# A two-layer decoder trunk: key choice of the first query half moved up, query rotation and four low parts on GpSimd, the first gate blocks as rounded products

## The reference

```python
for i in range(DEPTH):                                   # 2 layers
    p = x @ (w_in0 if i == 0 else w_in_rest[i - 1])      # attention, gates, r/k/v, LoRA inputs
    y_a = dsa_sparse_mqa(...)                            # below
    y_b = rwkv7_time_mix(...)                            # 4 rounds of 4 heads in the kernel
    g_a, g_b = jnp.split(jax.nn.sigmoid(p_gate + b_gate[i]), 2, axis=-1)
    x = layer_norm(alpha * x + (g_a * y_a + g_b * y_b) @ w_out[i], ...)
    x = layer_norm(alpha * x + conv_glu_ffn(x, ...), ...)

def dsa_sparse_mqa(...):
    c_q = rms_norm(cq_raw, g_cq)
    q = partial_rope((c_q @ w_uq).reshape(B, S, H_A, DH_A), *rope_a)      # 8 heads of 128, 32 rotated
    qi = partial_rope((c_q @ w_iq).reshape(B, S, H_IDX, D_IDX), *rope_i)  # 8 index heads of 64
    # per half of 128 queries:
    rel = jax.nn.relu(jnp.einsum('bqhd,bsd->bqhs', qib, ki))
    score = jnp.einsum('bqhs,bqh->bqs', rel, wib)        # weighted sum over the index heads
    _, idx = lax.top_k(score, 64)                        # the key choice
    # softmax attention over the chosen keys, heads of q against one shared k and v
```

## Time and profile before

| | |
|---|---|
| median of 3 runs | 1110.08 us (1109.13 to 1113.75) |
| the profiled execution | 1109.16 us, of it 1107.3 us from the first to the last instruction (span) |
| PE busy | 1077.9 us, 97% |
| DVE, ACT, POOL busy | 802.8, 570.7, 72.2 us |
| mean granted TensorE clock | 0.993 of full |
| PE's longest waits in sum | 4.6 us for the first load, 4.2 us for DVE in 2 layer norms, then 1.6 and less |

### The profile page before, as it was taken

One profiled execution on the slowest core, in us unless ns is written; L12 is line 12 of the kernel. 1 busy time (PEld: TensorE's weight loads), 2 busy tenths in 40 slices (PEclk: granted clock), 3 DMA queues, 4 the chain that ended last, 5 costly groups with the idle time before them and its releaser, 6 DMA issues. The chain is left out here.

```text
span 1107.3 us, 31915 instructions
## 1 busy us (share of the span) xinstructions
PE 1077.9 (97%) x13568; PEld 979.3 (88%) x13568; DVE 802.8 (72%) x1471; ACT 570.7 (52%) x1008; POOL 72.2 (7%) x61
## 2 busy tenths in 40 slices
PE   8999999999999999999999999999999999999996
PEld 8878888888897999998898888888888979999885
DVE  3678787878676877774557887878776778777645
ACT  3653555655444555553246445655565445555531
POOL 0000010101001000000100000101010010000001
PEclk9999999999999999999999999999999999999999
DMA  8533232322574666666374323222316646665661
GB/s 301 165 103 118 75 99 85 100 83 86 191 227 136 209 191 189 187 205 191 131 239 143 116 88 97 89 80 87 97 61 217 222 125 228 185 189 189 210 189 57
DMA packets 45527, 165.58 MB, mean 150 GB/s; under 512 B 5169, under 2 KB 5425, under 8 KB 45137
## 3 DMA queue, kind: packets, MB, share of 16 engines
q1 hardware_dynamic: 42736, 154.03, 43.3%
q0 software_dynamic: 1504, 7.47, 2.3%
q10 hardware_dynamic: 1152, 2.10, 0.6%
HBM read 160.44 MB, written 3.15 MB: 148 GB/s over the span
## 5 line engine op out<-in xcount | busy, mean ns | idle before, releaser
L771 PE MATMUL ps<-x_tok_r,mid_hi 128*128 128x256 f32 x576 | 176.5, 306 | 0.5 <-DVE ring_r L1753 0.5
L773 PE MATMUL ps<-x_tok_r,ring_r 128*128 128x256 f32 x576 | 162.2, 282 | 0.0
L772 PE MATMUL ps<-yb_hi,mid_hi 128*128 128x256 f32 x576 | 162.1, 281 | 0.0
L771 PEld LDWEIGHTS ps<-x_tok_r,mid_hi 128*128 128x128 f32 x576 | 108.6, 189 | 9.3 <-issue 1.4
L1753 DVE TENSOR_TENSOR ring_r<-ring,mid_hi 128x1024 fp32r<-128x1024 f32 x80 | 96.8, 1211 | 19.3 <-ACT mid_hi L1341 19.1
L772 PEld LDWEIGHTS ps<-yb_hi,mid_hi 128*128 128x128 f32 x576 | 108.9, 189 | 0.7 <-issue 0.7
L773 PEld LDWEIGHTS ps<-x_tok_r,ring_r 128*128 128x128 f32 x576 | 108.9, 189 | 0.0
L1341 ACT CAST mid_hi<-ring 128x1024 fp32r<-128x1024 f32 x80 | 83.8, 1047 | 36.5 <-PE ps L773 28.9
L2014 DVE TENSOR_TENSOR rs_ks_r<-ring,tha_kkn_r 128x1024 fp32r<-128x1024 f32 x44 | 53.9, 1225 | 21.5 <-ACT tha_kkn_r L1393 21.5
L2014 DVE TENSOR_TENSOR w_lo<-ring,w_hi 128x1024 fp32r<-128x1024 f32 x42 | 51.5, 1225 | 21.6 <-ACT w_hi L1393 21.5
L2014 DVE TENSOR_TENSOR vs_dC_r<-ring,b_k_r 128x1024 fp32r<-128x1024 f32 x44 | 53.7, 1220 | 17.1 <-ACT b_k_r L1393 17.1
(11 more groups left out here) (487 smaller groups left out, 3373.6 us busy)
## 6 DMA issues: line engine op xcount, KB each, us to landing
ring<-stream_dram SPq DMA_DIRECT2D x281, 512.0 KB, 3.7
lora_w<-lora_dram POOLq DMA_DIRECT2D x2, 1536.0 KB, 7.2
W_bt<-rpar_dram POOLq DMA_DIRECT2D x4, 512.0 KB, 5.7
kt_V<-rpar_dram POOLq DMA_DIRECT2D x4, 512.0 KB, 7.9
x_tok<-x_dram SPq DMA_DIRECT2D x2, 512.0 KB, 4.7
v_saved_dram<-vs_dC ACTq DMA_DIRECT2D x4, 256.0 KB, 4.3
x_tok<-x_dram SPq DMA_DIRECT2D x1, 1024.0 KB, 6.3
vf<-v_saved_dram ACTq DMA_DIRECT2D x4, 256.0 KB, 3.7
```

Of the source, the lines that this page charges most:

```text
L771: pe.matmul(dst, lh, rh, start=start, stop=False)
L772: pe.matmul(dst, lh, rl, start=False, stop=False)
L773: return pe.matmul(dst, ll, rh, start=False, stop=stop)
```

## The change

Four edits, all ahead of round 0 of each layer, and all in both layers.

1. The six first gate blocks are rounded products too. `MIDS` takes them in and `FIRST_MIDS` grows by six. With the last block of v (number 7 of the layer's rounded blocks) the gate blocks are numbers 8 to 13.
2. The low parts of numbers 7 to 10 (`POOL_LOWS`) are made by GpSimd (`low`), the rest by DVE.
3. The rotation of the queries (`queries(0)`, `queries(1)`) goes from DVE to GpSimd, between its low parts 8 and 9.
4. `topk(0)` stands right behind `s0` and `s1` on DVE, ahead of the sums of `s2` to `s5`. Into `topk(1)` go `rkv(l, 0, 2)`, `prep_decay`, `prep_pend`, `prep_ss`, `prep_rn` and a low part. Low part 13 stands between `prep_arc` and `prep_bk`.

```diff
-FIRST_MIDS = 2 + 3 * GB
+FIRST_MIDS = 2 + 3 * GB + 2 * GATES_FIRST
+POOL_LOWS = (7, 8, 9, 10)
...
-MIDS = [s for s in SLOTS if s[1] == "gate" and s[2] >= 2 * GATES_FIRST or s[1] == "rkv" and s[2] % KB >= GB
+MIDS = [s for s in SLOTS if s[1] == "gate" or s[1] == "rkv" and s[2] % KB >= GB
...
+            def low(l, m):
+
+                k = SLOT_AT[MIDS[l * MID_PER_LAYER + m]] % RING
+                pool.wait_ge(*act_mid(l, m))
+                pool.tensor_tensor(rounded["ring"][:, k, :], ring[:, k, :], f32(mid_hi[m % NM][:, :]), ALU.subtract
+                                   ).then_inc(*pool_mid.inc(l, m))
+
+            def queries(l, j):
+
+                pool.wait_ge(*act_att(l, f"q{j}"))
...
+                pool.tensor_tensor(t[0], x1, cos, ALU.mult)
+                pool.tensor_tensor(t[1], x2, sin, ALU.mult)
+                pool.tensor_tensor(t[2], x2, cos, ALU.mult)
+                pool.tensor_tensor(t[3], x1, sin, ALU.mult).then_inc(*pool_att.inc(l, f"rq{j}a"))
+                pool.wait_ge(*pool_att(l, f"rq{j}a"))
+                pool.tensor_tensor(x1, t[0], t[1], ALU.subtract)
+                pool.tensor_tensor(x2, t[2], t[3], ALU.add).then_inc(*pool_att.inc(l, f"rq{j}"))
...
+                low(l, 7)
+                low(l, 8)
+                queries(l, 0)
+                queries(l, 1)
+                low(l, 9)
+                low(l, 10)
                 head_norm(GROUPS * l)
...
-                pe.wait_ge(*dve_att(l, "rq1"))
+                pe.wait_ge(*pool_att(l, "rq1"))
...
-                topk(0)
-                prep_decay(r0)
-                prep_pend(r0)
-                prep_ss(r0)
-                topk(1, lambda: prep_rn(r0))
+                topk(1, {1: [lambda: rkv(l, 0, 2)], 5: [lambda: prep_decay(r0)],
+                         6: [lambda: prep_pend(r0), lambda: prep_ss(r0), lambda: mids_up_to(l, 12)],
+                         7: [lambda: prep_rn(r0)]})
+                mids_up_to(l, 13)
                 prep_keys(r0)
                 prep_keys_scaled(r0)
                 prep_arc(r0)
+                mids_up_to(l, 14)
                 prep_bk(r0)
```

More of the change, by code:

```diff
@@ L496, in trunk, with low_made @@
         act_mid = by_layer("act_mid", list(range(MID_PER_LAYER)))
-        dve_mid = by_layer("dve_mid", list(range(MID_PER_LAYER)))
+        dve_mid = by_layer("dve_mid", [m for m in range(MID_PER_LAYER) if m not in POOL_LOWS])
+        pool_mid = by_layer("pool_mid", list(POOL_LOWS))
+        def low_made(l, m):
+            return (pool_mid if m in POOL_LOWS else dve_mid)(l, m)
         mid_last = mid_gaps()
@@ L530, in trunk @@
         scores = lambda i: [f"s0{h}" for h in range(4 * i, 4 * i + 4)] if i < 2 else [f"s1{h}" for h in (2 * i - 4, 2 * i - 3)]
+        top = lambda t: ([f"causal{t}"] + sum([[f"max{t}{i}", f"rep{t}{i}"] for i in range(8)], [])
+                         + [f"sel{t}", f"selb{t}", f"keep{t}"])
         dve_att = Steps(sem("dve_att"), [["wi", "kst", "kmv"] + rope("rk") + ["cq", "kic", "ki"] + rope("rki") + rope("rqi")
-                                         + scores(0) + scores(1)
-                                         + (scores(2) + scores(3) + rope("rq0") + scores(4) + scores(5) + rope("rq1") if l else
-                                            rope("rq0") + scores(2) + scores(3) + rope("rq1") + scores(4) + scores(5))
-                                         + sum([[f"causal{t}"] + sum([[f"max{t}{i}", f"rep{t}{i}"] for i in range(8)], [])
-                                                + [f"sel{t}", f"selb{t}", f"keep{t}"] for t in range(TT)], [])
+                                         + scores(0) + scores(1) + top(0)
+                                         + scores(2) + scores(3) + scores(4) + scores(5) + top(1)
                                          + sum([[f"lh{g}", f"lg{g}", f"mx{g}", f"rc{g}", f"pn{g}"] for g in range(GROUPS)], [])
                                          for l in L2])
-        pool_att = by_layer("pool_att", ["eps", "rs"])
+        pool_att = by_layer("pool_att", ["eps", "rs"] + rope("rq0") + rope("rq1"))
         pe_prep = Steps(sem("pe_prep"), [(["ss", "zw", "za"] if r % GROUPS else ["zw", "za", "ss"]) + (["zv"] if r >= GROUPS else []) + ["rnT", "rnx"]
@@ L1604, in _ @@
                     index_turned()
+                    mids_up_to(l, 8)
                     scores_of(0)
                     scores_of(1)
+                    mids_up_to(l, 9)
                     queries(0)
@@ L1626, in _ @@
                 for i in range(1, GATES_FIRST):
+                    mids_up_to(l, 11 + 2 * i)
+                    mids_up_to(l, 12 + 2 * i)
                     gate(l, i)
-                    if i == 1:
-                        mids_up_to(l, FIRST_MIDS + 1)
+                mids_up_to(l, FIRST_MIDS + 1)
                 for g in range(GROUPS):
@@ L1748, in mids_up_to @@
             def mids_up_to(l, end):
-                for m in range(dve_mid.next - l * MID_PER_LAYER, min(end, MID_PER_LAYER)):
+                made = dve_mid.next - l * (MID_PER_LAYER - len(POOL_LOWS))
+                for m in [m for m in range(MID_PER_LAYER) if m not in POOL_LOWS][made:]:
+                    if m >= end:
+                        break
                     k = SLOT_AT[MIDS[l * MID_PER_LAYER + m]] % RING
@@ L2256, in scores_of, with topk @@
                         last.then_inc(*dve_att.inc(l, f"s{t}{h}"))
[L2258 to L2290 removed]
+                def topk(t, between={}):
                     dve.wait_ge(*dve_att(l, f"s{t}{H_IDX - 1}"))
@@ L2296, in topk @@
                     for i in range(TOPK // 8):
-                        if i == 5 and halfway:
-                            halfway()
+                        for step in between.get(i, []):
+                            step()
                         dve.wait_ge(*dve_att(l, f"causal{t}" if i == 0 else f"rep{t}{i - 1}"))
@@ L2310, in topk @@
                                       ).then_inc(*dve_att.inc(l, f"keep{t}"))
+                if l:
+                    shift_add(l, ("vres", 0), lora[:, 2:3, :], [26])
+                    index_queries()
+                    mids_up_to(l, 7)
+                    lora_w_low(1)
+                    rkv(l, 0, 1)
+                    lora_w_low(2)
+                    lora_low(2)
+                else:
+                    mids_up_to(l, 7)
+                    index_queries()
+                    lora_w_low(1)
+                    rkv(l, 0, 1)
+                scores_of(0)
+                scores_of(1)
+                topk(0)
+                for i in range(2, 6):
+                    scores_of(i)
                 def o_low(i):
```

56 lines of the change are left out of this document (15 added, 41 removed).

## The result

| | before | changed |
|---|---|---|
| median | 1110.38 us (6 runs, 1108.50 to 1113.83) | 1123.53 us (6 runs, 1120.71 to 1126.23) |
| ratio | | 1.0108, 95% interval 1.0089 to 1.0128 |
| profiled execution | 1109.16 us, span 1107.3 | 1126.23 us, span 1124.4 |
| mean granted clock | 0.993 | 0.990 |

The change makes the kernel about 1% slower; 1124.0 was forecast. So a difference is read between anchors on PE within one stretch, not between the two ends.

What follows compares the result with a forecast made beforehand. PE and DVE, arriving together at the grams 0.3 us apart, bound the kernel. Layer 1 +6.8, layer 0 +5.5, clock +1.7 make 14.0 on 1109.16: 1123.2, median 1124; forecast's own range 1118 to 1131, whole range 1111 to 1131.

Steps and rivals of the forecast that it cites:

- transposes late: Transposes of the queries ahead of round 0 start late: 7.6 us in layer 1, 0.4 in layer 0.
- `prep_1` behind ACT's copies: Layer 0: prep_1 waits to 76.7 for ACT's copies of the transposed queries, so PE stands 4.3 us.
- six blocks, at full clock: First gate blocks on PE: rounded 2.85 us against 3.55 in float32, saving 4.3 us per layer.
- `prep_rnT` behind the power: PE waits for head_norm's power on GpSimd, itself held by a DVE low part: +2.4 us layer 1, +3.2 layer 0.
- low part 13: PE's last gate block waits for DVE's keys, scaled keys, arc and this low part: +1.9 us in each layer.
- clock: Half level of 1.2 GHz after a long PE stand: one loss counted, layer 1's, 1.7 us, bounds 0 and 6.8.
- v: Layer 1: PE's 0.78 us wait for v behind the grams goes, since DVE is ahead by then: -0.8 us.
- The port: GpSimd and two-input DVE operations block each other; DVE's wait, not in the trace, taken as a whole GpSimd operation.
- GpSimd's prices: GpSimd's costs: a 1024-column low part 2.4 us (2.4 to 3.3), a 128-column rotation operation 0.45 (0.3 to 0.6).
- DVE never waits: Rival on the port: only GpSimd waits for DVE; layer 1 +2.4, layer 0 -0.2, time 1114 us; chance 0.13.
- nobody waits: Rival on the port: neither engine waits; layer 0 -2.0, layer 1 +1.0, time 1109 to 1111 us; chance 0.05.
- the blocks' saving arrives whole: Rival on the gate blocks: -4.3 us in both layers and the 0.8 wait gone, 1101 us; chance 0.03.

Runs made afterwards that it cites:

- the experiment with the port alone: Kernel before plus two unused GpSimd subtractions of 1024 columns per layer, one beside the score sums, one beside topk(0)'s MAX8 and MATCH_REPLACE8; 1110.22 us, one run.

## Why the prediction was right, step by step

| term, us | layer 1: forecast, measured | layer 0: forecast, measured |
|---|---|---|
| transposes late | 7.6, 6.0 | 0.4, 0.0 |
| `prep_1` behind ACT's copies | none | 4.3, 3.1 |
| six blocks, at full clock | -4.3, -3.4 | -4.3, -3.4 |
| `prep_rnT` behind the power | 2.4, 1.7 | 3.2, 0.9 |
| low part 13 | 1.9, 1.7 | 1.9, 1.7 |
| clock | 1.7, 2.8 | none, 2.6 |
| v | -0.8, -0.5 | none |

Measured they make 8.3 and 4.9 us, near the 8.3 and 5.1 between the anchors; forecast 14.0 with the clock, measured 13.2. Every wait came where it was named and ended with the engine that was named; only the stand ahead of the transposes was shorter than the 6 to 7 us named as its sign, 4.92. The sum is as good as it is because errors cancel: the lateness and the waits are 6.6 us smaller together, the saving of the blocks 1.8 and that of v 0.3 smaller, the clock 3.7 larger.

**The port** was the open step, and its direction was right: DVE does stand for the whole of a GpSimd low part (1.98 for an operation of 0.29, and the experiment with the port alone). The reading behind it was weaker than it says: the trace of before does have a case where DVE came second, a TENSOR_TENSOR at 305.14 that took its usual 1.22 beside a power of 8 columns (304.01 to 305.66). So it is the low parts for which DVE stands. And the first sum was taken for a two-input operation, which it is not; it waited all the same. Too much was made of it in one place: the rotation's small operations do not take strict turns with DVE's sums. The second rotation took 2.9 us and not 3.7. The seven sums of layer 0 lost 2.2 in all, 2.0 of it to low part 8 and next to nothing to the first rotation, so topk(0) was through 1.3 sooner than forecast (69.1 by before's clock, not 70.4), which is what `prep_1` came out smaller (1.2). In layer 1 topk(0) was only 0.3 sooner; of the 1.6 by which the transposes came out smaller, 0.8 lies in the rotation and the rest between topk(0) and ACT's copy.

**GpSimd's prices** held: a low part 2.35 to 2.40 (2.4 taken), a small operation 0.45 to 0.46 by itself (0.45 taken) and up to 0.64 beside DVE's sums. The Trainium skill, GPSIMD Engine Reference, section "Performance versus the Vector engine", led to an estimate of 2.25; the measured one is some 5% above it. Its advice against elementwise work on GpSimd fits half of the changed kernel: four of its eight low parts held DVE up by 1.5 us or more. The kernel that beat before makes six there, and one of them did.

**The blocks** were mis-sized: between small pieces a rounded block takes 2.96 to 3.04 us (637.79 to 640.75), not 2.85. The row of before that the 2.85 was read from gives 2.94 from start to start (49.68 to 52.62); the 0.09 taken off for a weight load stands in no row. Six save 3.4 a layer, not 4.3.

**The clock** was mis-sized, for two reasons. I counted one loss; there were two, 2.8 us in layer 1 (transposes 3.33 for 1.66 in layer 0, first block 4.11 for 2.96) and 2.6 in layer 0 (`prep_1` 1.57 for 0.9, block 1 4.87 for 2.96). And each was longer than the 1.7 read from the earlier trace rows. The rule that a loss hides in the stand behind it held by half. In the kernel with ACT's order changed, where layer 0 is the same code, `prep_1` waited 2.96, no row ran at the half level, and `prep_rnT` waited 2.31; here, with 2.6 lost, it waited 0.91, so 1.4 was hidden. The other half was not, since the power itself began 1.3 us later: a cast of ACT stood 3.48 us for PE's slow block (83.05), and behind that cast stands the exponential that the power's input needs. So the same stand of 3.0 us costs the clock in one execution and not in another: layer 0 is 5.1 and 5.0 us late where the rows were slow (the changed kernel, and the one with the copy alone moved), 3.8 where none was. With the cast alone moved it was 3.4, behind a stand of 2.46, and about half the rows of block 1 were slow. When the level falls behind a stand of this length is open.

**The rivals.** That DVE never waits is out by the port alone. That nobody waits, with it. That the blocks' saving arrives whole is out twice: by low part 13 in the changed kernel (1.65 us, so keys to low part do not fit into one block), and by the blocks alone, which cost 9 us a layer.

**Which edit costs what** was not in the prediction and is what the experiments add: the early topk(0) alone costs 10 us, the blocks alone 19, both with the work on GpSimd 13. No single place explains the 13 us. With ACT's two instructions moved the kernel is still 6.9 us above before. The last cut, with rotations, low parts, sums and key choice placed anew together, is 2.7 us below it; what each of its edits is worth was not measured.

## What to carry to other kernels

When two engines arrive together, taking work from one and giving it to the other moves nothing; work has to leave both, and it may go to GpSimd only beside DVE operations that don't hold or need the port, which a look at what DVE runs in those 2.4 us decides. Moving a long block ahead in one queue is priced by what stands behind it there and on the engine that waits for it (here a copy behind relus), not by the idle time that it fills. Read anchors within a stretch of one execution, and take several runs for the time: one run alone (1107.38) made a kernel that was no faster look 2.5 us faster.

## What was not expected of the hardware

- A DVE TENSOR_SCALAR with a single SBUF tensor as its input (L2293, fp32, SBUF to SBUF) stands for GpSimd as a two-input one does: 1.98 and 2.47 us for 0.29. The prediction had taken this row for an operation with two.
- DVE's SCALAR_TENSOR_TENSOR with one input in PSUM ran at its usual length beside a GpSimd low part: two in 0.86 us at 75.35, beside 74.33 to 76.69. MAX8 and MATCH_REPLACE8 too.
- Small operations on both sides interleave: GpSimd's 0.45 becomes 0.50 to 0.64, DVE's sums of 0.39 follow one another every 0.4 to 0.5.
- PE ran at the half level behind each stand of 3.27 us and more in these stretches, for 5 to 6 us in layer 0 of the changed kernel and in that with topk(0) alone; at 657.27 of the kernel with the blocks alone it did so only 1.1 us after it had started again. Below that the rows are mixed: behind 1.97 (the copy alone moved), 2.46 (the cast alone), 2.95, 2.98, 3.04 and 3.08 us it did, behind 2.15 (topk(0) alone), 2.31, 2.75 and 2.96 us it did not, and behind 1.90 us and less in none seen.
